# Four MiB of expert weights in other slots and at other points of the load queue, in a hybrid decoder block with a mixture of experts

## The chip, the core and the metric

The kernel runs on one core of one Trainium2 chip. Five engines work side by side and meet only at semaphores: PE (TensorE, matrix products), DVE (VectorE), ACT (ScalarE), POOL (GpSimd) and SP (SyncE, which here only issues transfers). SP and ACT each have a DMA queue of their own, q1 and q10 in the profile; both use the same 16 DMA engines. The metric is the device time in microseconds (us) of the core, median over runs.

## What is computed

One decoder block on 256 tokens of width 1024, float32: an input projection, a short convolution and an RWKV-7 mixer side by side, an output projection with a residual, then 32 experts of which each token takes four.

```python
xn = rmsnorm(h, norm_mix_g[l])
p = xn @ w_in[l]                                # 1024 x 8480
...
h = h + (gate_conv * y_conv + gate_rwkv * y_rwkv) @ w_out[l]
hn = rmsnorm(h, norm_ffn_g[l]).reshape(bsz * s, d)
h = h + moe_ffn(hn, router_w[l], router_b[l], exp_w1[l], exp_b1[l], exp_w2[l], exp_b2[l])
...
    u = xblk @ w1[e] + b1[e]                    # w1[e]: 1024 x 2048, 8 MiB
    return clamped_swiglu(u) @ w2[e] + b2[e]    # w2[e]: 1024 x 1024, 4 MiB
```

## The kernel before

Each engine has one program, in which waits on semaphores are written out. Weights pass through one SBUF tensor, `ring`, of 16 slots of 1 MiB each (128 partitions x 8 KiB). In the first part of the kernel the slots hold other things too: slots 0 to 5 are three buffers of two slots for chunks of the projection weights w_in and w_out; 6 and 7 hold the keys (`Kt`, `KK`), 8 to 11 further arrays of the mixer, 12 to 15 arrays and temporaries. The last chunk of w_in is in slots 0 and 1, the two chunks of w_out are in slots 4, 5 and 2, 3.

**Mixer and output projection.** PE works through 67 blocks of the input projection (`project`, L502; each one adds 1 to `blk_done`) with the pieces of the mixer between them (L588). Then follow four products of the output projection, `out_product(t, half)` at L886, t a half of the tokens and half a half of the columns, in the order (0,0), (0,1), (1,0), the turn of the first half of the residual sum (`turn_hb(0)`, L896), (1,1), then routing (L908 and on) and the first gather (L970, L971). The residual is the input x, loaded a second time: ACT asks for it at L1296, in two halves, right after norm_ffn_g at L1294. DVE waits for both halves of x (`xres_in`) before its first addition at L1825, and `turn_hb(0)` waits for that addition.

**Experts.** An expert is the 12 MiB of its w1 (two groups of four slots, j = 0 and 1) and its w2 (one group). The groups take the four places `GROUP = [8, 12, 4, 0]` of the ring in turn: expert 0 has w1 in slots 8 to 11 and 12 to 15 and w2 in 4 to 7, expert 1 begins with slots 0 to 3. PE runs experts one after the other: 64 matmuls at L995 for w1 (8 steps k of four slots' worth, each step frees one slot and adds 1 to `w_used`), 32 at L1030 for w2 (4 steps), and between them the combination of the previous expert (L959), the gather of the next (L950) and two turns (L1008, L1012). One turn of the loop is four experts, u = 0 to 3.

**Who loads.** SP issues every load of expert weights in one queue, in order, each behind a wait on `w_used`: a group is asked for when the steps that read its slots before are done. `load_expert` has L433 for a group of 4 MiB, L426 for two halves of 2 MiB where (u, j) is in `half_in`, and L441 for the two halves of w2. For the first expert PE adds to `w_used` by hand: 4 when the mixer's values are made and 4 when its results are merged (both right behind the last block of the input projection), and 8 when all four output products are done. PE waits for a whole group before its first step (`group_in`), and for the second half of a split group before k = 6.

Of the kernel before, what the change touches and what calls it, by code (L numbers as in the profile page):

```python
# [15 lines left out]
P = 128  # L16
# [5 lines left out]
E = 32  # L22
# [56 lines left out]
def build(nc, x, w_in, w_out, norm_ffn_g, norm_final_g, w2, a2, g2, router_w, router_b,  # L79
          exp_w1, exp_b1, exp_w2, exp_b2, params, consts, out):  # L80
    with ExitStack() as ctx:
        def sb(name, shape, dt=F32):
            return ctx.enter_context(nc.sbuf_tensor(name, shape, dt))

        def sem(name):
            return ctx.enter_context(nc.semaphore(name))
# [4 lines left out]
        ring = sb("ring", [P, 16, 2048])  # L91
# [57 lines left out]
        group_in = [sem(f"group_in{i}") for i in range(4)]  # L149
        w2_half_in = [sem(f"w2_half_in{i}") for i in range(4)]  # L150
        gfin_in = sem("gfin_in")
        half_in = {(1, 1): sem("refill_half_in"), (3, 1): sem("last_half_in")}
        last_sum = sem("last_sum")
        scaled_on_pool = sem("scaled_on_pool")
        merged = sem("merged")
# [21 lines left out]
        blk_done = sem("blk_done")  # L177
# [54 lines left out]
        w_used = sem("w_used")  # L232
# [24 lines left out]
        def chunk(n):  # L257
            s = 2 * LOADS[n]
            return ring[:, s:s + 2, :].rearrange("p s c -> p (s c)").rearrange("p (k c) -> p k c", k=KT)

        def chunk_in(n):

            parts = [len(stream[i]) if i < NIN else 1 for i in range(n + 1) if LOADS[i] == LOADS[n]]
            return slot_in[2 * LOADS[n]], 16 * sum(parts)

        def buffer_before(n):

            return max(i for i in range(n) if LOADS[i] == LOADS[n])


        blocks = [(0, 0, P), (0, P, P), (0, 2 * P, 32)]
# [29 lines left out]
        def blocks_until(n):  # L301

            return max(i for i, blk in enumerate(blocks) if blk[0] == n) + 1
# [17 lines left out]
        GROUP = [8, 12, 4, 0]  # L321

        def group(u, j):

            return (3 * u + j) % 4

        def slot(u, k):

            return GROUP[group(u, k // 4)] + k % 4

        def visits(u, j):

            return sum(group(a, b) == group(u, j) for a in range(u + 1) for b in range(3) if (a, b) <= (u, j))
# [43 lines left out]
        @block.sync  # L377
        def _(sp):
            for t in range(TT):
                sp.dma_start(flat(i_G2)[:, t * D:(t + 1) * D], x[0, t * P:(t + 1) * P, :]).then_inc(x_in[t], 16)  # L380
            sp.dma_start(cst[:, 0:P], consts[:, 0:P]).then_inc(const_in, 16)
            sp.dma_start(par[:], params).then_inc(const_in, 16)
            for n in range(NIN + 2):
                if n == NIN:
                    sp.wait_ge(dve_e[2], 11)
                    sp.wait_ge(dve_e[3], 11)
                elif n >= 3:
                    sp.wait_ge(blk_done, blocks_until(buffer_before(n)))
                s, _ = chunk_in(n)
                if n < NIN:  # L390
                    at = 0
                    for c0, width in stream[n]:
                        sp.dma_start(chunk(n)[:, :, at:at + width],
                                     w_in[0].rearrange("(k p) n -> p k n", p=P)[:, :, c0:c0 + width]).then_inc(s, 16)
                        at += width
                else:
                    c0 = (n - NIN) * CHUNK
                    sp.dma_start(chunk(n)[:, :, :],
                                 w_out[0].rearrange("(k p) n -> p k n", p=P)[:, :, c0:c0 + CHUNK]).then_inc(s, 16)
                if n == 1:  # L400

                    sp.dma_start(flat(i_GB)[0:64, 0:D], w2[0]).then_inc(lora_in, 16)
                    sp.dma_start(flat(i_GB)[64:128, 0:D], a2[0]).then_inc(lora_in, 16)
                    sp.dma_start(flat(i_GB)[:, D:2 * D], g2[0, 0:P]).then_inc(lora_in, 16)
                    tails = g2[0, P:P + 32].rearrange("r (h g c) -> r h g c", h=2, g=4)
                    for g in range(4):
                        sp.dma_start(flat(i_XI)[32 * g:32 * g + 32, 0:2 * P].rearrange("r (h c) -> r h c", h=2),
                                     tails[:, :, g, :]).then_inc(lora_in, 16)
                    sp.dma_start(left1[:, 0:NCONST - N_KEPT], consts[:, N_KEPT:NCONST]).then_inc(const_rest, 16)
                    sp.dma_start(cst[:, P:N_KEPT], consts[:, P:N_KEPT]).then_inc(const_rest, 16)  # L410
                if n == 2:
                    for s in range(3):
                        sp.dma_start(b1f[E * s:E * s + E, :], exp_b1[0]).then_inc(b1_in, 16)
                    for s in range(3):
                        sp.dma_start(b2f[E * s:E * s + E, :], exp_b2[0]).then_inc(b2_in, 16)

            def load_expert(e, it, u):

                for j in range(2):

                    if (u, j) in half_in:
                        rows_w1 = exp_w1[0, bass.ds(e, 1), 4 * P:8 * P, :].rearrange("a (p s) n -> p (a s) n", s=4)
                        for half, done in ((0, group_in[group(u, j)]), (1, half_in[u, j])):
                            sp.wait_ge(w_used, it * 12 + 6 + 2 * half)
                            g0 = GROUP[group(u, j)] + 2 * half
                            sp.dma_start(ring[:, g0:g0 + 2, :], rows_w1[:, 2 * half:2 * half + 2, :]).then_inc(done, 16)  # L426
                        continue
                    sp.wait_ge(w_used, it * 12 + 4 * j + 4)
                    src = exp_w1[0, bass.ds(e, 1), j * 4 * P:(j + 1) * 4 * P, :].rearrange(
                        "a (p s) n -> p (a s n)", s=4)  # L430
                    g = group(u, j)
                    dst = ring[:, GROUP[g]:GROUP[g] + 4, :].rearrange("p s n -> p (s n)")
                    sp.dma_start(dst, src).then_inc(group_in[g], 16)  # L433
                g = group(u, 2)
                for j in range(2):

                    sp.wait_ge(w_used, it * 12 + 2 * j + 10)
                    src = exp_w2[0, bass.ds(e, 1), j * 4 * P:(j + 1) * 4 * P, :].rearrange(
                        "a (p s) n -> p (a s n)", s=4)
                    dst = ring[:, GROUP[g] + 2 * j:GROUP[g] + 2 * j + 2, :].rearrange("p s n -> p (s n)")  # L440
                    sp.dma_start(dst, src).then_inc((group_in, w2_half_in)[j][g], 16)  # L441

            with sp.Fori(0, E // 4) as i:
                for u in range(4):
                    load_expert(i * 4 + u, i * 4 + u, u)
            sp.wait_ge(rounds_in, 1)
            n_rounds = sp.value_load(rounds[0:1, 0:1], min_val=1, max_val=4)
            with sp.If(n_rounds > 1):
                with sp.Fori(1, n_rounds) as r:
                    with sp.Fori(0, E // 4) as i:  # L450
                        for u in range(4):
                            load_expert(i * 4 + u, r * E + i * 4 + u, u)
            with sp.Else():
                sp.nop()
            for t in range(TT):
                sp.wait_ge(out_ready, t + 1)
                sp.dma_start(out[0, t * P:(t + 1) * P, :], HB[:, t, :]).then_inc(out_done, 16)
            sp.wait_ge(out_done, 16 * TT)
# [3 lines left out]
        def _(pe):  # L462
# [511 lines left out]
            def expert(r, i, u):  # L974

                it = r * E + i * 4 + u
                turn_no = r * (E // 4) + i
# [8 lines left out]
                last.then_inc(b1_used, 1)  # L986
                pe.wait_ge(xe_ready, it + 1)
                for k in range(8):
                    if k == 6 and (u, 1) in half_in:
                        pe.wait_ge(half_in[u, 1], turn_no * 16 + 16)  # L990
                    if k % 4 == 0:
                        pe.wait_ge(group_in[group(u, k // 4)], turn_no * 48 + 16 * visits(u, k // 4))
                    for part in range(2):
                        for half in range(2):
                            last = mm(ps[4 + part][64 * half:64 * half + 64, :], xe[:, k * CAP:(k + 1) * CAP],  # L995
                                      ring[:, slot(u, k), part * D + half * 512:part * D + half * 512 + 512],
                                      start=False, stop=k == 7)
                    last.then_inc(w_used, 1)
# [22 lines left out]
                for j in range(4):  # L1021
# [4 lines left out]
                    for i in range(2):  # L1026
                        k = 2 * j + i
# [934 lines left out]
```

## Time and profile before

| | |
|---|---|
| median of 3 runs | 1330.73 us (1323.72 to 1332.7) |
| the profiled execution: time, span | 1329.39 us, 1327.6 us |
| mean granted clock of TensorE | 0.98 |
| PE busy | 1223.7 us, 92% of the span |
| DVE, ACT, POOL busy | 304.0, 213.5, 58.9 us |
| moved by DMA | 450.03 MB, of it 403 MB expert weights |
| chain that ended last | PE 62%, DMA 32%, DVE 3% |
| of it expert weights (ring<-in_exp_w) | 30% |

Times in the rows are us from the start of the span, unless marked ns. The chain is followed back from the last instruction, at each step to what released it. A DMA row in a timeline is the issue on the queue (SPq, ACTq), not the transfer; the time from issue to landing stands apart. A DMA share of 1.00 means that all 16 engines are busy. PEclk is the clock that TensorE was granted, 1.00 being 2.4 GHz. "idle before <-X" says how long an engine stood still before a row and what ended it. A packet is one piece of a transfer on one DMA engine; the packets under 512 B here are the completion marks.

### The profile page before, as it was taken

The page shows a single profiled execution, that of the slowest core. Times are in us where ns is not written, and L with a number is a line of the kernel's source. Part 1 is how long each engine was busy: PE and PEld are TensorE (multiplying, and loading weights), DVE is VectorE, ACT ScalarE, POOL GpSimd, SP SyncE. Part 2 cuts the span into 40 slices and gives each one's busy share as a digit, 9 for nine tenths or more (in the row PEclk, how much of TensorE's full clock was granted, in tenths as well). Part 3 has the DMA queues.
Part 4 walks back from the last instruction along what each step waited for, and adds up shares of the span by engine and source line. Part 5 has one row for each costly group of instructions (what it writes and reads, how often), then busy time and mean ns, then how long its engine had stood idle before and what let it go on. Part 6 is the DMA issues. An engine that isn't in the chain of part 4 may idle for free.

```text
span 1327.6 us, 23606 instructions
## 1 busy us (share of the span) xinstructions
PE 1223.7 (92%) x10433; PEld 642.8 (48%) x10433; DVE 304.0 (23%) x598; ACT 213.5 (16%) x339; POOL 58.9 (4%) x33
## 2 busy tenths in 40 slices
PE   6999999999979999998989899898989989898996
PEld 5777888888653343333433333343333334343332
DVE  2364433233141121111211111121111111111113
ACT  4631221311031011000110000011100001010001
POOL 0800120000020000000000000000000000000000
PEclk9999999999989999999999999999999999999999
DMA  9511232245859999999999999999999999999994
GB/s 299 188 64 64 80 117 66 66 129 174 319 235 402 432 427 426 433 427 432 430 432 431 426 432 428 431 433 430 428 430 434 425 429 430 435 430 427 430 429 176
DMA packets 53925, 450.03 MB, mean 339 GB/s; under 512 B 5680, under 2 KB 23600, under 8 KB 35344
## 3 DMA queue, kind: packets, MB, share of 16 engines
q1 hardware_dynamic: 50880, 446.97, 81.3%
q10 hardware_dynamic: 2992, 2.25, 0.6%
q8 instruction: 46, 0.75, 0.2%
q14 instruction: 7, 0.06, 0.0%
HBM read 448.16 MB, written 1.05 MB: 338 GB/s over the span
## 4 chain that ended last, share of the span: by engine, by line
PE 62%; DMA 32%; DVE 3%; issue 1%; ACT 1%; SPq 0%; ACTq 0%; DVEq 0%
DMA ring<-in_exp_w 30%; PE ps L995 20%; PE ps L502 17%; PE ps L1030 10%; PE ps L588 4%; PE ps L959 3%; PE ps L950 2%; DMA work<-in_x 2%; PE ps L590 1%; PE ps L1008 1%; PE ps L983 1%; DVE work L1907 1%; PE ps L886 1%; PE ps L1017 1%; PE ps L1012 0%
## 5 line engine op out<-in xcount | busy, mean ns | idle before, releaser
L995 PE MATMUL ps<-ring,work 128*64 128x512 f32 x2048 | 465.1, 611 | 50.4 <-DMA ring<-in_exp_w 50.4
L995 PEld LDWEIGHTS ps<-ring,work 128*64 128x64 f32 x2048 | 159.0, 141 | 341.1 <-issue 286.8
L502 PE MATMUL ps<-work,ring 128*128 128x256 f32 (+1 forms) x1120 | 243.4, 384 | 0.8 <-ACT work L1068 0.8
L1030 PE MATMUL ps<-ring,work 128*64 128x512 f32 x1024 | 225.1, 592 | 0.0
L502 PEld LDWEIGHTS ps<-work,ring 128*128 128x128 f32 (+1 forms) x1120 | 200.2, 186 | 32.8 <-issue 3.5
L1347 ACT ACTIVATE work<-work 128x512 f32<-128x512 f32 x32 | 20.1, 629 | 732.2 <-DVE work L1896 732.2
L1896 DVE TENSOR_SCALAR work<-ps 128x512 f32<-128x512 f32 x32 | 22.1, 692 | 497.9 <-PE ps L995 497.9
L1030 PEld LDWEIGHTS ps<-ring,work 128*64 128x64 f32 x1024 | 72.5, 137 | 129.6 <-issue 129.5
L1912 DVE COPY work<-ps 128x512 f32<-128x512 f32 x32 | 22.1, 691 | 208.2 <-PE ps L1030 208.2
L950 PEld LDWEIGHTS ps<-sel,work 128*128 128x128 bf16 x1536 | 53.7, 118 | 24.2 <-issue 24.2
L959 PE MATMUL ps<-work 64*128 64x512 f32 x256 | 63.6, 615 | 0.0
L950 PE MATMUL ps<-sel,work 128*128 128x64 bf16 x1536 | 57.2, 198 | 0.0
L588 PE MATMUL ps<-ring 64*64 64x64 f32 x1600 | 46.3, 222 | 5.5 <-issue 5.5
L588 PEld LDWEIGHTS ps<-ring 64*64 64x64 f32 x1600 | 42.1, 136 | 10.1 <-issue 10.1
L1439 POOL TENSOR_TENSOR work<-work 128x1024 f32<-128x1024 f32 x1 | 3.3, 3256 | 918.3 <-DVE work L1924 918.3
L959 PEld LDWEIGHTS ps<-work 64*128 64x128 f32 x256 | 22.1, 186 | 41.0 <-issue 41.0
L1347 ACT ACT_TABLE_LOAD x32 | 41.1, 1283 | 2.1 <-issue 1.5
L1349 ACT ACTIVATE work<-ps 128x512 f32<-128x512 f32 x32 | 19.1, 597 | 72.8 <-PE ps L950 72.8
L886 PE MATMUL ps<-ring,work 128*128 128x512 f32 x64 | 29.0, 613 | 0.0
L1017 PE MATMUL ps<-work,oh 96*64 96x512 bf16 x64 | 13.0, 404 | 16.5 <-DVE work L1907 16.5
L588 PE MATMUL ps<-cst,ring 64*64 64x64 f32 x768 | 25.7, 220 | 0.0
L1486 DVE SCALAR_TENSOR_TENSOR ring<-ps,par,ring 128x255 f32<-128x255 f32 x24 | 11.6, 482 | 60.2 <-ACT ring L1085 59.8
(237 smaller groups left out, 749.1 us busy)
## 6 DMA issues: line engine op xcount, KB each, us to landing
ring<-in_exp_w SPq DMA_DIRECT2D x48, 4096.0 KB, 29.7
ring<-in_exp_w SPq DMA_DIRECT2D x96, 2048.0 KB, 30.3
ring<-in_w_in SPq DMA_DIRECT2D x8, 2048.0 KB, 8.9
ring<-in_w_in SPq DMA_DIRECT2D x16, 1024.0 KB, 7.3
ring<-in_w_out SPq DMA_DIRECT2D x2, 2048.0 KB, 10.8
ring<-in_w_in SPq DMA_DIRECT2D x1, 1152.0 KB, 7.2
work<-in_x SPq DMA_DIRECT2D x2, 512.0 KB, 4.0
work<-in_x ACTq DMA_DIRECT2D x2, 512.0 KB, 21.7
```

Source lines behind the costliest of these rows:

```text
L502: last = mm(bank_of(b)[width * g:width * g + width, 0:T], chunk(n)[:, k, c0:c0 + width], XN[:, k, :], start=k == 0, stop=k == KT - 1)
L588: last = mm(o, a(q, m), b_(q, m), start=True, stop=True)
L886: last = mm(ps[OUT[t][half]][:, :], Y[:, k, t * P:(t + 1) * P], chunk(NIN + half)[:, k, :], start=k == 0, stop=k == KT - 1)
L950: last = mm(ps[6][:, k * CAP:(k + 1) * CAP], H3[:, t, s, every_fourth(k)], sel[:, t, :], start=t + s == 0, stop=t + s == 3)
L959: last = mm(ps[2 * t + half][:, :], gts[64 * half:64 * half + 64, t * P:(t + 1) * P], yb[64 * half:64 * half + 64, :], start=False, stop=F ...
L995: last = mm(ps[4 + part][64 * half:64 * half + 64, :], xe[:, k * CAP:(k + 1) * CAP], ring[:, slot(u, k), part * D + half * 512:part * D + ...
L1017: last = mm(ps[7][64 * half:64 * half + 64, :], oh[:, :], b2s[:, half * 512:half * 512 + 512], start=True, stop=False)
L1030: last = mm(ps[7][64 * half:64 * half + 64, :], lhs, ring[:, slot(u, 8 + j), i * D + half * 512:i * D + half * 512 + 512], start=False, st ...
L1347: af(sig, glu, ACT.Sigmoid, scale=ALPHA).then_inc(sig_ready, 1)
L1349: af(xe, ps[6][:, :], ACT.Copy).then_inc(xe_ready, 1)
L1896: ts(glu, ps[4][:, :], LIMIT, None, ALU.min).then_inc(glu_ready, 1)
L1912: cp(yb, ps[7][:, :]).then_inc(y_ready, 1)
```

## The change

The order of the loads of the first two experts is written out, and two of them get other conditions:

- Expert 0's second half of w2, into slots 6 and 7 (the keys), is asked for right behind expert 0's w1, with no wait beyond `w_used` 8. Before, it stood behind `w_used` 16 like the first half, which keeps that wait.
- Expert 1's first group of w1, slots 0 to 3, is split in two halves. The first, slots 0 and 1, waits for the last block of the input projection (`blk_done` 67) and stands ahead of the wait for `w_used` 16; the second, slots 2 and 3, stays behind it.
- So that the split is the same in all turns of the loop, (1, 0) is added to `half_in`: in each turn expert u = 1 gets its first group as two loads of 2 MiB, each with its own wait, and PE waits for the second before k = 2.
- Experts 0 to 3 of SP's program are written out, and the loop starts at 1.

```diff
-        half_in = {(1, 1): sem("refill_half_in"), (3, 1): sem("last_half_in")}
+        half_in = {(1, 0): sem("second_half_in"), (1, 1): sem("refill_half_in"), (3, 1): sem("last_half_in")}
...
+            def load_expert(e, it, u, first_j=0):
+
+                for j in range(first_j, 2):
+
+                    if (u, j) in half_in:
+                        for half in range(2):
+                            sp.wait_ge(w_used, it * 12 + 4 * j + 2 + 2 * half)
+                            load_w1(e, u, j, half)
+                    else:
+                        sp.wait_ge(w_used, it * 12 + 4 * j + 4)
+                        load_w1(e, u, j)
                 for j in range(2):
...
                     sp.wait_ge(w_used, it * 12 + 2 * j + 10)
...
+                    load_w2(e, u, j)
+
+            sp.wait_ge(w_used, 4)
+            load_w1(0, 0, 0)
+            sp.wait_ge(w_used, 8)
+            load_w1(0, 0, 1)
+            load_w2(0, 0, 1)
+            sp.wait_ge(blk_done, len(blocks))
+            load_w1(1, 1, 0, 0)
+            sp.wait_ge(w_used, 16)
+            load_w2(0, 0, 0)
+            load_w1(1, 1, 0, 1)
+            load_expert(1, 1, 1, 1)
+            for u in range(2, 4):
+                load_expert(u, u, u)
+            with sp.Fori(1, E // 4) as i:
                 for u in range(4):
...
                 for k in range(8):
-                    if k == 6 and (u, 1) in half_in:
-                        pe.wait_ge(half_in[u, 1], turn_no * 16 + 16)
+                    if k % 4 == 2 and (u, k // 4) in half_in:
+                        pe.wait_ge(half_in[u, k // 4], turn_no * 16 + 16)
```

`load_w1` and `load_w2` issue the same transfers as before, a half of w1 with rows of 16 KiB per partition as L426 had.

SP's program behind the loads of w_out (L398), before the change. The wait stands in a row of its own (ISA) since the address is computed in the loop; 128x8192 is a group of 4 MiB, 128x4096 are 2 MiB:

```order
L398 DMA ring<-in_w_out 128x8x512 [waits blk_done]
L443 UNCONDITIONAL_BRANCH
L443 ISA
L433 ISA [waits w_used]
L433 DMA ring<-in_exp_w 128x8192
L428 REGISTER_ALU
L433 ISA [waits w_used]
L433 DMA ring<-in_exp_w 128x8192
L437 REGISTER_ALU
L441 ISA [waits w_used]
L441 DMA ring<-in_exp_w 128x4096
```

The same place in the changed program:

```order
L398 DMA ring<-in_w_out 128x8x512 [waits blk_done]
L423 DMA ring<-in_exp_w 128x8192 [waits w_used] x2
L436 DMA ring<-in_exp_w 128x4096
L427 DMA ring<-in_exp_w 128x4096 [waits blk_done]
L436 DMA ring<-in_exp_w 128x4096 [waits w_used]
L427 DMA ring<-in_exp_w 128x4096
L427 DMA ring<-in_exp_w 128x4096 [waits w_used] x2
```

Before, each load had a wait ahead of it, and the third, fourth and fifth all meant `w_used` of at least 16. Now one load (L436, w2's second half) has no wait of its own and one (L427) waits for the projection; both stand ahead of the wait that stands for the output projection.

PE's program at expert u = 1, before: the bias products, then the 16 matmuls of its first group.

```order
L983 MATMUL ps<-work,oh 64x512 [waits oh_ready,u_free]
L983 MATMUL ps<-work,oh 64x512 x3
L995 MATMUL ps<-ring,work 64x512 [waits group_in3,xe_ready]
L995 MATMUL ps<-ring,work 64x512 x15
```

And changed, up to its second group:

```order
L1007 MATMUL ps<-work,oh 64x512 [waits oh_ready,u_free]
L1007 MATMUL ps<-work,oh 64x512 x3
L1019 MATMUL ps<-ring,work 64x512 [waits group_in3,xe_ready]
L1019 MATMUL ps<-ring,work 64x512 x7
L1019 MATMUL ps<-ring,work 64x512 [waits second_half_in]
L1019 MATMUL ps<-ring,work 64x512 x7
```

The group's 16 matmuls are the same; a wait for its second half now stands in their middle. PE's lines are 24 higher than before.

## Rows read from the trace of the kernel before

**Rows 1.** PE's waits for expert weights: us in total, times, longest us.
```profile
PE ps L995 <- DMA ring<-in_exp_w: 50.4, 25, 2.7
```

**Rows 2.** The experts' stage: stretch, us, busy us (instructions) by engine, PEclk, DMA share, GB/s.
```profile
531.79:1269.03 737.24, 673.96 (x4134) 268.11 (x4129) 119.26 (x252) 76.73 (x100) 0.00 (x0) 0.98 1.00 430
```

**Rows 3.** The chain that ended last, in order of time: start us, us, what.
```profile
350.17 22.06 DMA work<-in_x
...
398.29 15.35 PE ps L995 x64
...
426.29 13.73 PE ps L995 x64
...
452.67 13.73 PE ps L995 x64
...
538.84 28.09 DMA ring<-in_exp_w
...
1178.84 31.62 DMA ring<-in_exp_w
```

**Rows 4.** Timeline of SP's queue: start us, us, line, operation, count.
```profile
345.39 1.00 SPq L433 DMA_DIRECT2D ring<-in_exp_w  x2
...
383.50 0.91 SPq L441 DMA_DIRECT2D ring<-in_exp_w  x2
...
384.70 0.33 SPq L433 DMA_DIRECT2D ring<-in_exp_w  x1
...
403.54 4.17 SPq L426 DMA_DIRECT2D ring<-in_exp_w  x2
...
410.40 3.75 SPq L441 DMA_DIRECT2D ring<-in_exp_w  x2
...
426.03 7.63 SPq L433 DMA_DIRECT2D ring<-in_exp_w  x2
```

**Rows 5.** Landings of L433's loads issued before 380, and of the one at 384.7.
```profile
DMA to landing us min/median/max: 12.9/18.6/24.4
...
DMA to landing us min/median/max: 22.2/22.2/22.2
```

**Rows 6.** Stretches between and behind the loads, columns as in rows 2.
```profile
372.00:383.00 11.00, 9.41 (x24) 4.90 (x25) 4.02 (x6) 5.33 (x7) 2.76 (x2) 0.84 0.00 0
...
426.00:428.50 2.50, 2.50 (x16) 0.88 (x14) 0.79 (x2) 0.00 (x0) 0.00 (x0) 1.00 0.84 256
```

**Rows 7.** ACT's queue at 349, and issue to landing of norm_ffn_g and x.
```profile
349.30 0.34 ACTq L1294 DMA_DIRECT2D work<-in_norm_ffn_g  x1
...
349.67 1.00 ACTq L1296 DMA_DIRECT2D work<-in_x  x2
...
DMA to landing us min/median/max: 15.9/15.9/15.9
...
DMA to landing us min/median/max: 21.3/21.7/22.1
```

**Rows 8.** Timeline ahead of expert 0; in brackets the idle time before.
```profile
349.02 20.76 PE L886 MATMUL ps<-ring,work 128*128 128x512 f32 x48
...
372.25 1.29 DVE L1825 TENSOR_TENSOR work<-work,ps 128x512 f32<-128x512 f32 x2 [21.60 <-DMA work<-in_x]
...
373.59 1.62 PE L896 MATMUL ps<-cst,work 128*128 128x128 f32 x8 [3.81 <-DVE work L1825]
...
375.00 8.23 PE L886 MATMUL ps<-ring,work 128*128 128x512 f32 x16
```

**Rows 9.** Packets by queue, 353 to 368.5, then 368.5 to 372.3: count, MB, share.
```profile
q1 hardware_dynamic: 192, 5.77, 87.7%
...
q10 hardware_dynamic: 190, 0.71, 12.3%
...
q10 hardware_dynamic: 242, 0.86, 56.3%
```

**Rows 10.** The granted clock after the idle time, columns as in rows 2.
```profile
374.00:378.00 4.00, 4.00 (x12) 2.28 (x11) 2.24 (x4) 2.91 (x6) 0.00 (x0) 0.57 0.00 0
```

More of the change, by code:

```diff
@@ L415, in _, with load_w1 @@
                         sp.dma_start(b2f[E * s:E * s + E, :], exp_b2[0]).then_inc(b2_in, 16)
-            def load_expert(e, it, u):
-                for j in range(2):
-                    if (u, j) in half_in:
[L422 to L434, printed above, removed]
+            def load_w1(e, u, j, half=None):
+                src = exp_w1[0, bass.ds(e, 1), j * 4 * P:(j + 1) * 4 * P, :]
+                g = group(u, j)
+                if half is None:
+                    dst = ring[:, GROUP[g]:GROUP[g] + 4, :].rearrange("p s n -> p (s n)")
+                    sp.dma_start(dst, src.rearrange("a (p s) n -> p (a s n)", s=4)).then_inc(group_in[g], 16)
+                else:
+                    g0 = GROUP[g] + 2 * half
+                    rows_w1 = src.rearrange("a (p s) n -> p (a s) n", s=4)
+                    sp.dma_start(ring[:, g0:g0 + 2, :], rows_w1[:, 2 * half:2 * half + 2, :]).then_inc(
+                        half_in[u, j] if half else group_in[g], 16)
@@ new lines, in load_w2 @@
+            def load_w2(e, u, j):
+                g = group(u, 2)
+                src = exp_w2[0, bass.ds(e, 1), j * 4 * P:(j + 1) * 4 * P, :].rearrange(
+                    "a (p s) n -> p (a s n)", s=4)
+                dst = ring[:, GROUP[g] + 2 * j:GROUP[g] + 2 * j + 2, :].rearrange("p s n -> p (s n)")
+                sp.dma_start(dst, src).then_inc((group_in, w2_half_in)[j][g], 16)
+            def load_expert(e, it, u, first_j=0):
+                for j in range(first_j, 2):
+                    if (u, j) in half_in:
+                        for half in range(2):
+                            sp.wait_ge(w_used, it * 12 + 4 * j + 2 + 2 * half)
+                            load_w1(e, u, j, half)
+                    else:
+                        sp.wait_ge(w_used, it * 12 + 4 * j + 4)
+                        load_w1(e, u, j)
@@ L435, in load_expert @@
                 for j in range(2):
                     sp.wait_ge(w_used, it * 12 + 2 * j + 10)
[L438 to L443, printed above, removed]
+                    load_w2(e, u, j)
```

## The prediction

> **What bounds the kernel now.** I read the stages first, then who asks for expert weights and when, then what stands just ahead of the first expert. PE is busy nearly everywhere, but from the sixth expert on it waits for weights, 25 times, 50.4 us in all [rows 1]. The stage from the sixth expert to the middle of the last but one [rows 2] shows why: the DMA share is 1.00 and the rate 430 GB/s over 737 us. An expert is 12 MiB (12.58 MB), so 29.2 us of DMA; PE alone needs 26.4 us (two successive experts that nothing holds start at 426.29 and 452.67 in the chain [rows 3]). From 538.84 on the chain goes again and again through 28 to 32 us of "DMA ring<-in_exp_w" and then PE [rows 3]. The end is therefore the time at which the unbroken stream of weights begins, plus its bytes over 430 GB/s, plus a PE tail. The question is only what the change does to that beginning.
>
> When does it begin? The ring holds 16 MiB. SP asks for 8 MiB at 345.39, for 8 more at 383.50 and 384.70, and then has nowhere to put anything until expert 0 has used slots: 403.54, 407.4, 410.40 and 413.8, 2 MiB each, and 4 MiB at 426.03 [rows 4]. The ring is full at 384.70 + 22.2 = 406.9 [rows 5], 3.4 us after the first refill is asked for. The four refills are 8.39 MB, 19.5 us at 430 GB/s, so they end near 426; there, over 426 to 428.5, the rate falls to 256 GB/s [rows 6]. The DMA queue is then dry, and **the request of 426.03 starts the unbroken stream**. It is a release by PE, 27.7 us after expert 0 starts at 398.29 [rows 3]. All that was loaded ahead of it leaves no trace in the end time.
>
> **Part 1: 4 MiB are asked for earlier.** They take 4.19 MB / 430 = 9.75 us from what is asked for at 383.5, and there is room for them: from 372 to 383 the rate is 0 [rows 6]. The ring would be full nearly 10 us earlier. But the first refill still waits for expert 0's second k step, and the four refills still end before the request of 426.03, which PE sets as before. Value: 0. This is the choice that matters most: the gap is filled and opens again behind the ring. The cover is the ring's full 16 MiB against a PE that starts at 398; were PE's start earlier than 393, the part would be worth something.
>
> **Part 2: what shares the DMA engines with them.** ACT asks at 349.30 for norm_ffn_g (512 KB) and at 349.67 and 350.2 for x, two times 512 KB [rows 7]. DVE's first add of the residual (L1825) needs both halves of x. It sits idle 21.6 us for them and starts at 372.25; PE has run out of work at 349.02 + 20.76 = 369.8 and is idle 3.81 us before it can turn the sum [rows 8]. The chain has the same: 22.06 us of "DMA work<-in_x" stand in it ahead of expert 0 [rows 3]. So x is on the path that sets expert 0's start.
>
> Why does 1 MiB take 22 us? The packets say it. From 353 to 368.5 the SP queue (q1) sends 192 packets and the ACT queue (q10) 190: one for one, while q1 carries 5.77 MB and q10 0.71 MB. As soon as q1's data is through, q10 sends 242 packets, 0.86 MB, within 3.8 us [rows 9]. A q1 packet of 32 KB (8 MiB in 256 packets, 16 on each of 16 engines) lets one q10 packet of 4 KB by. When q1 is empty, 242 / 16 = 15 packets an engine are still to go in q10: 13 of data, 2 completions.
>
> Now the change. Behind the 8 MiB SP adds 2 MiB of w2 at once (it waits for nothing new, so at about 346.4) and 2 MiB of w1 when the last projection block is done; PE goes on to the output projection at 349.02 [rows 8], so that is about when x is asked for, and long before q1 would be empty at 368.5. On each DMA engine these are 16 packets of 16 KB. The 15 q10 packets must alternate with them. Two of q1's 15 turns are its own completion packets (after the first 8 MiB and after w2) and weigh nothing; 13 are data. A packet of 16 KB takes 16384 B / (430/16 GB/s) = 0.61 us [rows 2]. **x lands 13 x 0.61 = 7.9 us later**, near 380.1. Bounds: 0 if q10 is not held, and 9.75 if x goes last.
>
> The Trainium skill (DMA: Bandwidth & Descriptors, Queues, rings and completion order) also has the engines go round between queue rows at packet granularity, but with some 9 to 17 descriptors drained from one row before the switch. By that rule the eight pieces of one of ACT's transfers would leave in a single turn, norm_ffn_g soon after 358 and only the last half of x behind 2 MiB, 4.9 us late instead of 7.9. The trace speaks against it: norm_ffn_g lands 15.9 us after its issue, at 365.2 [rows 7].
>
> **Part 3: what follows from 7.9 us.** From the add at 372.25 to expert 0 (398.29) runs one chain of DVE, PE, ACT and POOL work with no DMA in it that changes; it moves as a block. PE's idle grows from 3.8 to 11.7 us. w_used reaches 16 at about 391.4 instead of 383.5; the 4 MiB left then are in by about 403, ahead of their use (expert 0 reaches w2 only after its 15.35 us of L995, at 421.6 or later, and expert 1 starts 28 us after expert 0 [rows 3]). Expert 0 starts at 406.2, the first refill is asked for at 411.4, the request that starts the stream at 433.9. The DMA engines stand still from about 403 to 412, again a gap that costs nothing of its own. The stream is as long as before, so the end moves by 7.9 us.
>
> **Part 4: the clock.** After today's idle the granted clock is 0.57 of full over 374 to 378 [rows 10], the lower level of 1.2 GHz for most of it, and 16 matmuls of L886 take 8.23 us where 48 take 20.76, that is 6.92 per 16 [rows 8]: 1.3 us already paid. A longer idle may pay nothing more, or, if the low level holds through all 16, 13.84 - 8.23 = 5.6 us more. The row is nearest to what is paid now, since work of the same kind brought the clock back within 4 us; I take 0. The mean granted clock of the whole execution is 0.98, so no other stage has much of it to lose.
>
> **Part 5: the rest.** SP's first four experts are written out: some more rows in its program, on an engine that computes nothing and waits nearly always. Expert u=1's first group comes as two loads in every turn of the loop: 8 more issues of 0.33 us on SP. Its packets become 16 KB, as those of w2 already are, at the same rate. The request can go out two k steps earlier, but in the stream a load lands 28 to 32 us after its request [rows 3], so the queue is deep and an earlier request buys nothing. PE gets one wait more per four experts, behind it only that expert's k = 2; it can only be let go earlier than by the wait for the whole group. All 0. Nothing in the last two experts changes: they are u=2 and u=3.
>
> **Sum.** 7.9 + 0 + 0 + 0. The profiled execution is 1329.39 us (span 1327.6), so 1337.3; the median of the runs shown is 1.3 us above it, so **1338.6 us**, +0.6%.
>
> **Rivals.**
> - No change, 1330.7: x is not held longer, because the ACT queue gets past 16 KB packets. For it: only 1.57 MB are concerned. Against it: one-for-one packets [rows 9]. 0.13.
> - Faster, 1321.0: the 9.75 us do reach the stream. Its place is the request at 426.03: there would have to be 9.75 us of work queued at that moment. It decides only if the four refills are not through by then, and the dip to 256 GB/s says they are [rows 6]. 0.04.
> - Whole transfers by turns: an ACT transfer's eight packets go together, so the last of x waits for eight packets of 16 KB, 8 x 0.61 = 4.9 us: 1335.6. Then norm_ffn_g, asked for while the first 4 MiB were under way, would have landed soon after these (345.39 + 12.9 = 358.3 [rows 5]); it landed at 349.30 + 15.9 = 365.2 [rows 7]. 0.05.
> - Clearly slower, by the clock: the 11.7 us of idle leave PE at 1.2 GHz through turn and L886, 7.9 + 5.6 = 13.5: 1344.2. It decides once the low level lasts past some 7 us of work. 0.08.
> - The forecast: 0.70.
>
> **How the numbers follow.** A measurement of this kernel can tell about 1% (13.3 us) from no change. The range has to hold the forecast, no change and the clock rival, so 1329 to 1345; outside is the faster rival and some of the scatter (the runs before span 1323.7 to 1332.7). None of the cases is faster by 1%: 0.02 for scatter. The clock rival and a little scatter are slower by over 1%: 0.11. The rest, 0.87, within 1%.
>
> **What would show it.** DVE's wait at the first residual add should be 29 to 30 us instead of 21.6, PE's idle before the turn of the residual 11 to 12 us, expert 0's first L995 row (now another line number) at 405 to 407, DMA silent before the first refill, and PE's waits for expert weights again about 50 us. In the packets, q10 should go one for one with q1 until about 379. The prediction is wrong if x lands before 376, if the rate just ahead of the 4 MiB request for expert 2 (433.9) shows no dip, or if the stream's rate differs from 430 GB/s.

## The result and the profile after

| | before | after |
|---|---|---|
| median of 8 runs each | 1330.17 us (1323.72 to 1332.7) | 1337.49 us (1334.94 to 1340.22) |
| ratio, 95% interval | | 1.0059 [1.0043, 1.0075] |
| profiled execution: span | 1327.6 us | 1335.0 us |

The kernel became 0.6% slower, 7.3 us between the medians. The forecast was 1338.6 us, +0.6%, with 1329 to 1345 around it.

SP's queue in the changed kernel, to be held against [rows 4]:

```profile
344.15 0.82 SPq L423 DMA_DIRECT2D ring<-in_exp_w  x2
...
345.02 0.43 SPq L436 DMA_DIRECT2D ring<-in_exp_w  x1
...
348.13 0.33 SPq L427 DMA_DIRECT2D ring<-in_exp_w  x1
...
389.08 0.33 SPq L436 DMA_DIRECT2D ring<-in_exp_w  x1
...
389.45 23.09 SPq L427 DMA_DIRECT2D ring<-in_exp_w  x3
...
415.64 3.76 SPq L436 DMA_DIRECT2D ring<-in_exp_w  x2
...
431.28 7.63 SPq L423 DMA_DIRECT2D ring<-in_exp_w  x2
```

The early 4 MiB are in the queue at 345.02 (L436, w2's second half) and 348.13 (L427, the first half of expert 1's first group). What the output projection has to release follows at 389.08, the request for expert 2 at 431.28, 5.25 us later than before. (The row at 389.45 also holds the first two refills, asked for at 408.8 and 412.2.)

The timeline ahead of expert 0, against [rows 8], and the first expert in the chain, against [rows 3]:

```profile
347.94 20.76 PE L910 MATMUL ps<-ring,work 128*128 128x512 f32 x48
...
378.27 1.29 DVE L1849 TENSOR_TENSOR work<-work,ps 128x512 f32<-128x512 f32 x2 [28.70 <-DMA work<-in_x]
...
379.62 1.97 PE L920 MATMUL ps<-cst,work 128*128 128x128 f32 x8 [10.91 <-DVE work L1849]
...
381.38 7.58 PE L910 MATMUL ps<-ring,work 128*128 128x512 f32 x16
...
349.11 29.14 DMA work<-in_x
...
404.02 15.02 PE ps L1019 x64
```

DVE waits 28.70 us for x instead of 21.60, PE stands idle 10.91 us instead of 3.81. Both grew by 7.1 us, and the chain shows the transfer of x with 29.14 us where it had 22.06.

The packets by queue from 353 to 368.5 and from 368.5 to 381 (count, MB, share of the 16 engines), against [rows 9], and the landing of x:

```profile
q1 hardware_dynamic: 213, 5.59, 84.7%
...
q10 hardware_dynamic: 216, 0.82, 13.2%
...
q1 hardware_dynamic: 267, 3.85, 72.0%
...
q10 hardware_dynamic: 205, 0.71, 13.9%
...
DMA to landing us min/median/max: 23.5/26.3/29.1
```

In the second stretch q10 had 0.86 MB to move within 3.8 us and nobody beside it. Now q1 goes on with 3.85 MB, and q10's 205 packets go in between. (The counts include 16 completion marks for each transfer.) The second half of x lands 29.1 us after its issue.

Three stretches, columns as in [rows 2]: while x is still under way, between the full ring and the first refill, and from the request for expert 2 on.

```profile
374.00:378.00 4.00, 0.00 (x0) 0.00 (x0) 0.00 (x0) 0.00 (x0) 0.00 (x0) 0.50 1.00 426
...
404.00:410.00 6.00, 6.00 (x26) 1.93 (x26) 0.26 (x1) 2.24 (x3) 2.12 (x1) 0.80 0.17 47
...
431.25:433.75 2.50, 2.50 (x16) 0.92 (x14) 0.89 (x2) 0.00 (x0) 0.00 (x0) 1.00 0.86 269
```

Where the DMA engines had moved nothing in 372 to 383 [rows 6], they are full at 374. The hole is now behind the ring: its last load lands at 389.45 + 13.3 = 402.8, the first refill is asked for at 408.8, and from 404 to 410 the rate is 47 GB/s. At the request for expert 2 the rate dips to 269 GB/s, as it did to 256 [rows 6]. From there the stream is what it was: PE waits for it 50.9 us in all.

```profile
PE ps L1019 <- DMA ring<-in_exp_w: 50.9, 25, 2.9
...
537.05:1276.00 738.95, 675.71 (x4136) 264.20 (x4134) 119.41 (x252) 76.75 (x100) 0.00 (x0) 0.98 1.01 430
```

### The profile page after: what moved, and what is told of

Same layout as the page of the kernel before. It is cut to its first block, busy times and chain, and to the rows that moved or that the text cites. A ratio compares the mean times of both kernels' runs of the same rounds, so it can differ in the third digit from the quotient of the medians.

```text
span 1335.0 us, 23579 instructions
## 1 busy us (share of the span) xinstructions
PE 1225.4 (92%) x10433; PEld 638.5 (48%) x10433; DVE 303.0 (23%) x598; ACT 213.7 (16%) x339; POOL 54.8 (4%) x33
## 4 chain that ended last, share of the span: by engine, by line
PE 62%; DMA 33%; DVE 3%; issue 1%; ACT 1%; SPq 0%; ACTq 0%; DVEq 0%
DMA ring<-in_exp_w 30%; PE ps L1019 20%; PE ps L526 17%; PE ps L1054 10%; PE ps L612 4%; PE ps L983 3%; DMA work<-in_x 3%; PE ps L974 2%; PE ps L614 1%; PE ps L1032 1%; DVE work L1931 1%; PE ps L1007 1%; PE ps L1041 1%; PE ps L910 1%; PE ps L1036 0%
## 5 line engine op out<-in xcount | busy, mean ns | idle before, releaser
L1019 PE MATMUL ps<-ring,work 128*64 128x512 f32 x2048 | 466.1, 612 | 50.9 <-DMA ring<-in_exp_w 50.9
L1019 PEld LDWEIGHTS ps<-ring,work 128*64 128x64 f32 x2048 | 154.7, 141 | 347.1 <-issue 293.1
L1920 DVE TENSOR_SCALAR work<-ps 128x512 f32<-128x512 f32 x32 | 22.1, 692 | 499.7 <-PE ps L1019 499.7
L1054 PEld LDWEIGHTS ps<-ring,work 128*64 128x64 f32 x1024 | 72.5, 136 | 129.6 <-issue 129.5
L1936 DVE COPY work<-ps 128x512 f32<-128x512 f32 x32 | 22.1, 691 | 208.2 <-PE ps L1054 208.2
L910 PE MATMUL ps<-ring,work 128*128 128x512 f32 x64 | 28.3, 601 | 0.0
## 6 DMA issues: line engine op xcount, KB each, us to landing
work<-in_x ACTq DMA_DIRECT2D x2, 512.0 KB, 26.3
```

Source lines behind the costliest of these rows:

```text
L910: last = mm(ps[OUT[t][half]][:, :], Y[:, k, t * P:(t + 1) * P], chunk(NIN + half)[:, k, :], start=k == 0, stop=k == KT - 1)
L1054: last = mm(ps[7][64 * half:64 * half + 64, :], lhs, ring[:, slot(u, 8 + j), i * D + half * 512:i * D + half * 512 + 512], start=False, st ...
L1920: ts(glu, ps[4][:, :], LIMIT, None, ALU.min).then_inc(glu_ready, 1)
L1936: cp(yb, ps[7][:, :]).then_inc(y_ready, 1)
```

## The experiments

All ratios are to the kernel before, measured on the same chip in the same rounds. The diffs are cuts that show the loads; where a run leaves the split out, its line of `half_in` is that of before.

**split_only.** The change without its early loads: do the split of expert 1's group and the written-out experts cost anything?

```diff
             load_w1(0, 0, 1)
-            load_w2(0, 0, 1)
-            sp.wait_ge(blk_done, len(blocks))
-            load_w1(1, 1, 0, 0)
             sp.wait_ge(w_used, 16)
             load_w2(0, 0, 0)
+            load_w2(0, 0, 1)
+            load_w1(1, 1, 0, 0)
             load_w1(1, 1, 0, 1)
```

> The changed kernel with its four early-or-late loads put back behind the output projection (w_used 16); the split of expert 1's first group in every turn of the loop and the four written-out experts stay. If the 4 MiB ahead of the residual x are the whole cause, DVE waits 21.6 us for x as before, PE is idle 3.8 us, and the time is that of before, 1330.2 us (ratio 1.000, within 0.15%). If the split itself costs something, as the stream of the changed kernel suggests (the 819.0 us between the landings of expert 3's and expert 31's last w2 half became 821.1), the ratio is 1.0016, and the same stretch again takes 821 us.

Measured: ratio 1.0000 [0.9987, 1.0013], wait for x 21.3 us, PE idle 3.5 us. So all of the loss sits in the two early loads. The stretch between the two landings took 819.6 us, between the 819.0 of before and the 821.1 of the changed kernel; see after_again.

**hold_for_x.** The changed kernel, in which the early 4 MiB must let x go first.

```diff
             load_w1(0, 0, 1)
+            sp.wait_ge(xres_in, 16 * TT)
             load_w2(0, 0, 1)
             sp.wait_ge(blk_done, len(blocks))
             load_w1(1, 1, 0, 0)
```

> The changed kernel, with SP made to wait for both halves of the residual x (landed) ahead of the early 4 MiB. They are still asked for some 11 us before the output projection is done. If x is what costs and the 4 MiB in themselves are worth nothing, x's wait is again 21.6 us and the ratio to the kernel before is 1.000 (up to 1.0016 if the split costs 2 us). If the early 4 MiB are worth their 9.75 us of transfer once x is out of their way, the ratio is 0.993. If neither x but the mere queueing hurts, it stays at 1.006.

Measured: 0.9998 [0.9985, 1.0011]. The waits, SP's queue and the DMA rate of this kernel:

```profile
DVE work L1850 <- DMA work<-in_x: 21.3, 1, 21.3
...
370.94 0.33 SPq L436 DMA_DIRECT2D ring<-in_exp_w  x1
...
371.31 0.43 SPq L427 DMA_DIRECT2D ring<-in_exp_w  x1
...
383.01 0.33 SPq L436 DMA_DIRECT2D ring<-in_exp_w  x1
...
372.00:376.00 4.00, 3.71 (x11) 2.68 (x12) 1.77 (x4) 3.21 (x5) 0.00 (x0) 0.50 0.95 352
...
398.00:404.00 6.00, 6.00 (x22) 1.78 (x22) 0.18 (x1) 2.24 (x3) 2.12 (x1) 0.70 0.19 63
```

The two loads still go out 12 us ahead of the output projection's end (370.94 and 371.31 against 383.01) and fill the hole (352 GB/s where it was 0), and x is on time. The loss is gone, and no gain has come: 63 GB/s from 398 to 404 say where it went. Both halves of the argument, that x costs all of it and that the early 4 MiB are worth nothing, are in this one run. Its interval reaches down to 2.0 us less than before; the worth of the 4 MiB by bytes alone would be 9.75.

**w2_only.** Half of the early bytes: 2 MiB of w2, without the split.

```diff
             load_w1(0, 0, 1)
             load_w2(0, 0, 1)
-            sp.wait_ge(blk_done, len(blocks))
-            load_w1(1, 1, 0, 0)
             sp.wait_ge(w_used, 16)
             load_w2(0, 0, 0)
-            load_w1(1, 1, 0, 1)
+            load_w1(1, 1, 0)
```

> The kernel before, with only expert 0's second half of w2 (2 MiB, packets of 16 KB) asked for right behind its w1; no split, nothing else. If the queues go one packet for one packet, q10's 15 remaining turns meet 8 data packets of 0.61 us and then an empty q1: x lands 4.9 us later, the wait is 26.5 us, ratio 1.0037 minus what the clock gives. Of the changed kernel's 7.1 us that would be two thirds for half of the bytes. If x simply waited for its share by bytes, half the bytes would cost half, 3.5 us (wait 25.1, ratio 1.0027).

Measured: 1.0038 [1.0026, 1.0051], wait for x 26.3 us. Against the 21.3 us of split_only, half of the bytes add 5.0 us to the wait and all of them, in the changed kernel, 7.4 us. That is the order that the count of packets gives: eight of 16 KB per engine meet x here, and in the changed kernel not sixteen but the 13 that go by before q10 is empty. The traces have both counts. These are q1's rows up to the end of x, in w2_only from 371 to 379.2 and in the changed kernel from 367.1 to 377.1; in both stretches its packets are of 16 KB, with 32 completion marks:

```profile
q1 hardware_dynamic: 160, 2.10, 60.3%
...
q1 hardware_dynamic: 238, 3.38, 79.1%
```

Without the marks they are 128 and 206 packets, 8.0 and 12.9 an engine.

**w2_small.** The same 2 MiB at the same place, as four transfers whose pieces are single rows of w2 (4 KB) instead of four rows (16 KB). PE waits for them once before the experts.

```diff
-            load_w2(0, 0, 1)
+            for q in range(4):
+                sp.dma_start(ring[:, 6 + q // 2, (q % 2) * D:(q % 2) * D + D],
+                             exp_w2[0, 0, 4 * P:8 * P, :].rearrange("(p s) n -> p s n", s=4)[:, q, :]).then_inc(
+                                 w2_half_in[2] if q == 3 else quarters_in, 16)
```

> w2_only with the early 2 MiB in four transfers whose packets are 4 KB instead of 16 KB (the same bytes to the same place). One packet for one packet: q10's 15 turns meet packets of 0.15 us, 15 x 0.15 = 2.3 us, so DVE waits 23.6 us for x (w2_only: 26.3) and the ratio is about 1.0015. If x waits for the bytes that are queued and not for packets, the wait stays at 26.3 us and the ratio at 1.0038.

Measured: 1.0012 [1.0000, 1.0024]. DVE's and PE's waits, w2_only first, then w2_small (the row of PE's weight load, PEld, has 0.8 us more than PE's own idle time):

```profile
DVE work L1847 <- DMA work<-in_x: 26.3, 1, 26.3
...
PEld ps L918 <- DVE work L1847: 9.3, 1, 9.3
```

```profile
DVE work L1852 <- DMA work<-in_x: 23.3, 1, 23.3
...
PEld ps L922 <- DVE work L1852: 6.3, 1, 6.3
```

23.3 us instead of 26.3 with the same bytes queued at the same time. What x pays for is the size of the packets that it alternates with, not the bytes ahead of it.

**x_first.** If x is on the path, the 8 MiB of loads that hold it up already before the change should let it by. This is the kernel before with its first loads written out and one wait added.

```diff
             sp.wait_ge(w_used, 8)
+            sp.wait_ge(xres_in, 16 * TT)
             load_w1(0, 0, 1)
             sp.wait_ge(w_used, 16)
             load_w2(0, 0, 0)
             load_w2(0, 0, 1)
             load_w1(1, 1, 0)
```

> The kernel before, with one wait added: SP asks for expert 0's second 4 MiB of w1 only when the residual x has landed; what stands behind the output projection stays there. Only 8 packets an engine of q1 are then ahead of or beside x, so x lands near 361 instead of 372, before PE has finished its three products at 369.8. PE's idle of 3.8 us goes, and with it the dip of the clock (1.3 us in L886 and 0.5 in the turn). The stream starts 5.5 us earlier: ratio 0.996. If something else holds the first expert (routing, the weights), the ratio is 1.000; if the later w1 is not in time (it lands near 373, expert 0 starts at 393) it is over 1.

Measured: 0.9958 [0.9943, 0.9974]; 1323.82 us against 1330.36 for the kernel before in the same rounds. The landing of x, DVE's wait, and PE ahead of the experts:

```profile
DMA to landing us min/median/max: 10.7/11.1/11.5
...
DVE work L1848 <- DMA work<-in_x: 11.1, 1, 11.1
...
349.88 20.76 PE L909 MATMUL ps<-ring,work 128*128 128x512 f32 x48
...
370.48 1.04 PE L919 MATMUL ps<-cst,work 128*128 128x128 f32 x8
...
371.35 7.03 PE L909 MATMUL ps<-ring,work 128*128 128x512 f32 x16
...
393.44 15.02 PE ps L1018 x64
```

x takes 11.5 us instead of 22.1. PE goes from its three products (349.88 + 20.76 = 370.6) straight into the turn, which takes 1.04 us, and the fourth product 7.03 us instead of 8.23: idle time and dip of the clock are gone together.

**x_first_early.** The change on top of that, with nothing left that it could harm.

```diff
             sp.wait_ge(xres_in, 16 * TT)
             load_w1(0, 0, 1)
+            load_w2(0, 0, 1)
+            sp.wait_ge(blk_done, len(blocks))
+            load_w1(1, 1, 0, 0)
             sp.wait_ge(w_used, 16)
             load_w2(0, 0, 0)
-            load_w2(0, 0, 1)
-            load_w1(1, 1, 0)
+            load_w1(1, 1, 0, 1)
```

> x_first with the change on top: behind the landing of x come expert 0's second w1 group, then the early 4 MiB, split as in the changed kernel. x is out of the way, so this is the cleanest value of the early 4 MiB. Theory: 0, since the stream of weights starts at the request for expert 2, a release by PE; the ratio is that of x_first, 0.996 (0.9965 with half a microsecond for the split). If the early transfer counts, 0.989.

Measured: 0.9959 [0.9945, 0.9973], the same as x_first's 0.9958. The 4 MiB are worth nothing here either, to within some 3 us by the two intervals; had their 9.75 us counted, 0.989 was expected.

**after_again.** The changed kernel once more.

> The changed kernel once more, for a second profile. DVE's wait for x 28 to 29 us, ratio 1.006. The stretch from expert 3's to expert 31's last landing was 821.1 us in its first profile, against 819.0 to 819.3 without the split and 819.6 to 819.8 with the split alone. If that is the early loads' doing, it is 821 again; if scatter, it is 819.5 to 820.

Measured: 1.0056 [1.0042, 1.0069], wait for x 28.6 us, PE idle 10.9 us. The long stretch took 819.8 us this time. So the 821.1 of the first profile was scatter for the greater part. Without the split the profiles of the kernel before, w2_only and x_first have 819.0, 819.2 and 819.3 us; with it split_only, hold_for_x, x_first_early and after_again have 819.6 to 819.8. That half microsecond, if it is the split's, cannot be told in the times (split_only 1.0000). w2_small, without the split, had 819.7, so it may be scatter as well.

**What the profiles share.** The mixer ahead of all this ends at times that differ by up to 3.8 us between profiles of kernels that do the same up to there (PE's first L886, or its later line number, starts between 347.94 and 351.71). Counted from that start, the request for expert 2 comes:

| kernel | wait for x | L886 to request for expert 2 | against before | ratio measured |
|---|---|---|---|---|
| before | 21.6 | 426.03 - 349.02 = 77.0 | | 1 |
| split_only | 21.3 | 76.9 | -0.2 | 1.0000 |
| hold_for_x | 21.3 | 77.9 | +0.8 | 0.9998 |
| w2_small | 23.3 | 78.4 | +1.4 | 1.0012 |
| w2_only | 26.3 | 81.0 | +4.0 | 1.0038 |
| after | 28.7 | 83.3 | +6.3 | 1.0059 |
| after_again | 28.6 | 84.7 | +7.7 | 1.0056 |
| x_first | 11.1 | 70.8 | -6.2 | 0.9958 |
| x_first_early | 11.1 | 71.3 | -5.7 | 0.9959 |

One part in a thousand is 1.33 us: 1.0038 is 5.1 us, 1.0059 is 7.8, 0.9958 is -5.6. In all eight other profiles the measured time moved as this one interval did, within about 1.5 us (the interval is from one profile each, the ratio from 5 to 12 executions).

## Why the prediction was right

**The bound (the stream starts at the request for expert 2).** Right. The table above is its test: none, 2 or 4 MiB asked for early leave no trace in the time unless they move the request itself.

**Part 1, the early 4 MiB are worth 0.** Right, shown twice, in hold_for_x and in x_first_early. In both the ring is full earlier and the DMA engines then nearly stand still, at 63 GB/s in the one and 83 GB/s in the other. The rows of x_first_early, while the 4 MiB are under way and behind the ring:

```profile
376.00:380.00 4.00, 4.00 (x18) 2.37 (x17) 0.69 (x1) 1.44 (x2) 2.83 (x2) 1.00 1.00 430
...
395.00:400.00 5.00, 5.00 (x20) 1.52 (x18) 0.00 (x0) 1.74 (x2) 1.69 (x1) 0.78 0.22 83
```

**Part 2, x lands 7.9 us later.** The mechanism is right, shown by w2_small and by the two counts at w2_only; the size was a little high. DVE's wait grew by 7.1 us (28.7 and 28.6 against 21.6, or by 7.4 against the 21.3 of split_only and hold_for_x). The term counted 13 data packets of q1 beside the last 15 turns of q10, at 0.61 us each. The count came out (12.9), and in w2_only, where it is eight, 8 x 0.61 = 4.9 us stands against 4.7 to 5.0 measured. Why thirteen cost 0.5 to 0.8 us less than 7.9 no run shows. One candidate, not tested: before, q10 alone kept the engines busy for only 56.3% of its last 3.8 us [rows 9], so a part of the added packets' time may fall where they stood still.

The rule of whole transfers by turns would have had x 4.9 us late with both loads. The 7.1 us speak against it, and so does w2_only: by turns x would wait for the same eight packets there as in the changed kernel, so both would lose the same, where 5.0 and 7.4 us were measured. The equal counts of [rows 9] do not decide this by themselves, since a 4 MiB load and a half of x both have eight data packets and one mark on each engine. Short stretches of the kernel before do. From 365.5 to 366.7, the time of one 32 KB packet, each queue sends one packet an engine; from 363.1 to 364.3 q10's 16 are mostly completion marks (14 of them, 0.01 MB); and from 357 to 358.2, where 16 of q1's 31 are the marks of the first 4 MiB, q10 sends 32:

```profile
q1 hardware_dynamic: 16, 0.52, 101.1%
q10 hardware_dynamic: 16, 0.07, 13.2%
...
q1 hardware_dynamic: 16, 0.52, 104.6%
q10 hardware_dynamic: 16, 0.01, 2.3%
...
q1 hardware_dynamic: 31, 0.49, 100.2%
q10 hardware_dynamic: 32, 0.13, 37.1%
```

Of the Trainium skill (DMA: Bandwidth & Descriptors, Queues, rings and completion order) the round between the queue rows stands; the 9 to 17 descriptors in a row do not for these two queues: the stretches show them changing over after each single one.

**Part 3, everything behind the add moves as a block.** Right within a microsecond. From the add to the start of expert 0 it took 26.04 us before and 404.02 - 378.27 = 25.75 us after. That expert 0 started at 404.0 in this profile and not at the 406.2 of the forecast (405 to 407 as a sign) comes from the mixer, which ended 1.08 us earlier, from x (0.8) and from this chain (0.3); in after_again it started at 405.2. The two other signs came out just below what was written as well: DVE's wait 28.7 us (29 to 30), PE's idle time 10.91 (11 to 12).

**Part 4, the clock costs nothing more.** Right. PE was idle three times as long, and its clock was at 0.50, the level of 1.2 GHz, over all of 374 to 378. The work came back at 379.6, and over 382 to 386 the mean was 0.94 again (0.67 in after_again). From the start of the turn to the end of the fourth product it took 9.6 us before, 9.3 and 10.3 in the two profiles of the changed kernel, 9.7 and 10.6 in split_only and hold_for_x, whose idle was 3.5 us, and 9.4 in w2_only with 8.5 us of idle: no order by the length of the idle time. Without any, in x_first, it is 7.9. The two slowest, hold_for_x and after_again:

```profile
372.29 1.97 PE L921 MATMUL ps<-cst,work 128*128 128x128 f32 x8 [3.52 <-DVE work L1850]
...
374.04 8.84 PE L911 MATMUL ps<-ring,work 128*128 128x512 f32 x16
...
379.83 1.97 PE L920 MATMUL ps<-cst,work 128*128 128x128 f32 x8 [10.86 <-DVE work L1849]
...
381.60 8.55 PE L910 MATMUL ps<-ring,work 128*128 128x512 f32 x16
```

So the stretch pays 1.4 to 2.7 us for PE having been idle at all. The forecast had that as "1.3 us already paid", for the product alone.

**Part 5, the rest at 0.** Right: split_only 1.0000.

**The sum.** 7.9 forecast. In the profile: 7.1 for x, -1.1 for the mixer, about -0.3 in the chain to expert 0 and -0.5 from there to the request for expert 2, which makes the 5.25 us by which the request for expert 2 is later, and 2.1 in the stream, of which after_again shows no more than 0.8. So the single profile's 7.4 is x's 7.1 with pieces of scatter that nearly cancel; the ratio, 7.8 us with its interval from 5.7 to 10, and after_again's 1.0056, 7.4 us, carry the result. The forecast of 1338.6 is 1.1 us above the median: 0.6 of that is the median of before, 1330.17 and not 1330.73, the rest x's share. So close an agreement is in part luck, since the ratio's interval is 4 us wide.

**The rivals.** No change fell with the later landing of x, the faster one with the dip to 269 GB/s and the two runs for Part 1, the turns with Part 2, and the clock rival with L910's 7.58 and 8.55 us, where it had 13.84.

## What to carry to other kernels

A hole in the DMA timeline is worth filling only if something that waits for DMA is on the other side of it; here the ring was full and the next request was PE's to make, so the hole only moved. Before queueing large loads early, look for the small load on another queue that the path waits for: as long as both queues have work, it pays one large packet for each of its own, so either it goes first or the large load's pieces are made small. Here one wait on the small load's semaphore, ahead of half of the bulk that was already there, gained 0.4%.

## What the runs showed of the hardware

- Two hardware queues on the same 16 DMA engines alternate by single packets whatever their size: 4 KB of q10 against 32 KB of q1, so q10 gets 0.71 of 6.48 MB [rows 9]. Cutting the other queue's packets from 16 to 4 KB brought a waiting 1 MiB forward by 3.0 us at the same bytes.
- A completion mark takes a turn like any other packet: while q1 sends 16 of them, q10 gets 32 packets through instead of 16, and while q10 sends 14, q1 still sends a 32 KB packet on each engine (kernel before, 357 to 358.2 and 363.1 to 364.3).
- A longer idle time of TensorE, 10.9 us instead of 3.5 to 3.8, cost nothing more at the start of the next work: 9.3 and 10.3 us against 9.6, 9.7 and 10.6 for the same 24 matmuls, and 7.9 with no idle time.
